# Eight weight chunks in other column orders, and weight slots 64 bytes further apart

## What is computed

```python
h = rms_norm(x, g_mix[l])
proj = h @ w_in[l]
q, k, v, z, f, scal, gates = jnp.split(proj, SPLIT_POINTS, axis=-1)
...
gate_a, gate_f = jnp.split(jax.nn.sigmoid(gates), N_BRANCHES, axis=-1)
x = x + (gate_a * y_a + gate_f * y_f) @ w_o[l]
```

## Time and profile before

| | before |
|---|---|
| median of 2 runs | 2401.64 us (2400.94 to 2402.33) |
| profiled execution, its span | 2400.5 us |
| TensorE busy | 2376.3 us, 99% |
| VectorE busy | 1773.2 us, 74% |
| ScalarE busy | 1027.0 us, 43% |
| GpSimd busy | 267.3 us, 11% |
| DMA | 475.16 MB, 198 GB/s on average |

### The profile page before, as it was taken

One profiled execution on the slowest core, in us unless ns is written; L12 is line 12 of the kernel. 1 busy time (PEld: TensorE's weight loads), 2 busy tenths in 40 slices (PEclk: granted clock), 3 DMA queues, 4 the chain that ended last, 5 costly groups with the idle time before them and its releaser, 6 DMA issues.

```text
span 2400.5 us, 29952 instructions
## 1 busy us (share of the span) xinstructions
PE 2376.3 (99%) x12546; PEld 1946.3 (81%) x12546; DVE 1773.2 (74%) x2054; ACT 1027.0 (43%) x849; POOL 267.3 (11%) x226
## 2 busy tenths in 40 slices
PE   8999999999999999999999999999999999999998
PEld 7888888878888888888888888777777788888886
DVE  6585568557697887786766789989999967458865
ACT  5453345334344544444444435444434444544432
POOL 1002201210000000000000000055555400000000
PEclk9999999999999999999999999999999999999999
DMA  7343354347655555555555556665556586566753
GB/s 264 136 167 133 141 185 166 118 155 259 259 193 189 195 194 211 194 193 193 193 193 193 193 210 217 203 237 186 193 192 201 180 299 241 184 231 236 258 195 140
DMA packets 84230, 475.16 MB, mean 198 GB/s; under 512 B 8704, under 2 KB 8832, under 8 KB 32512
## 3 DMA queue, kind: packets, MB, share of 16 engines
q1 hardware_dynamic: 84096, 473.25, 55.7%
HBM read 450.15 MB, written 23.07 MB: 197 GB/s over the span
## 4 chain that ended last, share of the span: by engine, by line
PE 90%; DVE 6%; DMA 2%; issue 1%; ACT 1%; DVEq 0%; SPq 0%; ACTq 0%
PE acc L2179 28%; PE acc L2182 27%; PE acc L2185 27%; PE banks L2324 2%; DVE w_lo L1257 1%; PE banks L2373 1%; DMA raw<-in_w 1%; DVE convT L1577 1%; DVE padT L1304 1%; PE banks L2440 1%; PE banks L2453 1%; ACT w_hi L796 1%; PE banks L2196 0%; PE banks L2493 0%; PE banks L2475 0%
## 5 line engine op out<-in xcount | busy, mean ns | idle before, releaser
L1257 DVE TENSOR_TENSOR w_lo<-raw,w_hi 128x2048 fp32r<-128x2048 f32 x394 | 909.1, 2309 | 387.2 <-ACT w_hi L796 384.2
L796 ACT ACTIVATE w_hi<-raw 128x2048 fp32r<-128x2048 f32 x394 | 752.6, 1915 | 667.6 <-DMA raw<-in_w 667.2
L2179 PE MATMUL acc<-w_hi,a_hi 128*128 128x512 f32 x2112 | 839.5, 397 | 5.8 <-DVE w_lo L1257 2.6
L2182 PE MATMUL acc<-w_lo,a_hi 128*128 128x512 f32 x2112 | 824.9, 391 | 0.0
L2185 PE MATMUL acc<-w_hi,a_lo 128*128 128x512 f32 x2112 | 824.4, 390 | 0.0
L2179 PEld LDWEIGHTS acc<-w_hi,a_hi 128*128 128x128 f32 x2112 | 397.4, 188 | 105.6 <-issue 16.9
L2185 PEld LDWEIGHTS acc<-w_hi,a_lo 128*128 128x128 f32 x2112 | 397.4, 188 | 84.9 <-DVE a_lo L1293 0.3
L2182 PEld LDWEIGHTS acc<-w_lo,a_hi 128*128 128x128 f32 x2112 | 397.8, 188 | 78.6
L2179 PE MATMUL acc<-w_hi,b_hi 128*128 128x512 f32 x928 | 361.8, 390 | 0.0
L2185 PE MATMUL acc<-w_hi,b_lo 128*128 128x512 f32 x928 | 361.3, 389 | 0.0
L2182 PE MATMUL acc<-w_lo,b_hi 128*128 128x512 f32 x928 | 361.2, 389 | 0.0
(11 more groups left out here) (354 smaller groups left out, 1688.9 us busy)
## 6 DMA issues: line engine op xcount, KB each, us to landing
raw<-in_w SPq DMA_DIRECT2D x395, 1024.0 KB, 4.8
spilled<-stage SPq DMA_DIRECT2D x72, 256.0 KB, 5.8
gate_in<-spilled SPq DMA_DIRECT2D x20, 512.0 KB, 5.7
x_rows<-in_x SPq DMA_DIRECT2D x4, 512.0 KB, 8.5
x_rows<-in_x SPq DMA_DIRECT2D x1, 2048.0 KB, 9.3
mem_rows<-in_mem SPq DMA_DIRECT2D x2, 1024.0 KB, 6.6
spilled<-stage_b SPq DMA_DIRECT2D x8, 256.0 KB, 5.8
out<-y_rows SPq DMA_DIRECT2D x3, 512.0 KB, 2.7
```

Source lines behind the costliest of these rows:

```text
L796: act.activation(w_hi[:, n % HIGH, :], raw[:, n % RAW, :], ACT.Copy)\
L1257: dve.tensor_tensor(w_lo[:, n % RAW, :], raw[:, n % RAW, :], w_hi[:, n % HIGH, :].bitcast(F32), ALU.subtract).then_inc(lo_split, 1)
L2179: pe.matmul(o, hi[:, tk], wh, start=first, stop=False)
L2182: pe.matmul(o, hi[:, tk], wl, start=False, stop=False)
```

## The change

Eight chunks, all of w_gate_f and w_gate_a, get another order of their columns within a unit, made on the host by `laid_in_blocks`. TensorE reads them with an access pattern that undoes it (`moving`), so that the result stands in `acc` in the old order. What ScalarE, VectorE and the DMA do to a unit is as before. With a block of i elements, block b of slice k starts at element 4 i b + i k of the unit, so one slice is read as 512 / i runs of i elements, and the starts of two runs are 4 i elements apart.

| chunk | w_gate_f 0 | 1 | 2 | 3 | w_gate_a 0 | 1 | 2 | 3 |
|---|---|---|---|---|---|---|---|---|
| order | 32 | 2 | halves | back | 1 | 64 | 256 | 16 |
| one slice is read as | 16 runs of 32, 512 bytes apart | 256 pairs, 32 bytes apart | elements 0, 256, 1, 257, ... | 512 elements with step -1 | 512 elements, 16 bytes apart | 8 runs of 64 | 2 runs of 256 | 32 runs of 16, 256 bytes apart |

In the second part the slots of `raw`, `w_lo` and `w_hi` become 2064 elements long, of which 2048 are used, so that they begin 8256 bytes apart. All that is allocated behind them moves up by up to 512 bytes per partition.

```diff
+BLOCKS = {("w_gate_f", 0): 32, ("w_gate_f", 1): 2, ("w_gate_f", 2): "halves", ("w_gate_f", 3): "back",
+          ("w_gate_a", 0): 1, ("w_gate_a", 1): 64, ("w_gate_a", 2): 256, ("w_gate_a", 3): 16}
...
-        ctx.enter_context(nc.sbuf_tensor("arena", [P, 52984], F32))
+        ctx.enter_context(nc.sbuf_tensor("arena", [P, 53112], F32))
...
-        raw = take("raw", [P, RAW, UE])
-        w_lo = at("w_lo", 0, [P, RAW, UE], F32R)
-        w_hi = take("w_hi", [P, HIGH, UE], F32R)
+        raw = take("raw", [P, RAW, UE + 16])[:, :, 0:UE]
+        w_lo = at("w_lo", 0, [P, RAW, UE + 16], F32R)[:, :, 0:UE]
+        w_hi = take("w_hi", [P, HIGH, UE + 16], F32R)[:, :, 0:UE]
...
-                    wh = w_hi[:, n % HIGH, k * NW:(k + 1) * NW]
-                    wl = w_lo[:, n % RAW, k * NW:(k + 1) * NW]
+                    wh = moving(w_hi[:, n % HIGH, :], k, block_order(name, col))
+                    wl = moving(w_lo[:, n % RAW, :], k, block_order(name, col))
...
+def block_order(name, n):
+
+    return BLOCKS.get((name, n))
+
+
+def moving(x, k, block):
+
+    if block is None:
+        return x[:, k * NW:(k + 1) * NW]
+    if block == "back":
+        return x[:, (k + 1) * NW - 1:k * NW - 1 if k else None:-1]
+    if block == "halves":
+        return x[:, k * NW:(k + 1) * NW].rearrange("p (z j) -> p j z", z=2)
+    return x.rearrange("p (b k i) -> p k b i", k=KU, i=block)[:, k]
+
+
+def laid_in_blocks(units, block):
+
+    u = units.reshape(-1, P, KU, NW)
+    if block == "back":
+        return np.ascontiguousarray(u[:, :, :, ::-1]).reshape(units.shape)
+    if block == "halves":
+        return np.ascontiguousarray(u.reshape(-1, P, KU, NW // 2, 2).swapaxes(3, 4)).reshape(units.shape)
+    return np.ascontiguousarray(u.reshape(-1, P, KU, NW // block, block).swapaxes(2, 3)).reshape(units.shape)
...
-    w = np.concatenate([units[name][n * u:(n + 1) * u] for name, n, u, _ in CHUNKS])
+    piece = lambda name, n, u: units[name][n * u:(n + 1) * u]
+    w = np.concatenate([piece(name, n, u) if block_order(name, n) is None else
+                        laid_in_blocks(piece(name, n, u), block_order(name, n)) for name, n, u, _ in CHUNKS])
```

More of the change, by code:

```diff
@@ L399, in region @@
         def region(name, kb, shape, dt=F32):
-            assert dr + kb * KB + int(np.prod(shape[1:])) * 4 <= 52984 * 4, name
+            assert dr + kb * KB + int(np.prod(shape[1:])) * 4 <= 53112 * 4, name
             return at(name, dr + kb * KB, shape, dt)
```

## The result

| | before | after |
|---|---|---|
| median | 2401.64 us | 2475.84 us (2474.19 to 2477.48, 2 runs) |
| ratio | | 1.0308, 95% interval 1.0291 to 1.0325 |
| span of the profiled execution | 2400.5 us | 2475.7 us |

What follows compares the result with a forecast made beforehand. TensorE, busy 2376.3 of 2400.5 us, was taken to bound the kernel. Pairs at +18.9 us, single elements and halves at +58.2 each, all else 0, summed to +135.3 on 2401.6: 2537 us, range 2420 to 2580.

Steps and rivals of the forecast that it cites:

- (a): Slots of raw, w_lo and w_hi 8256 bytes apart instead of 8192: taken as 0 us.
- 13.4 ns left over per matmul: Weight matmuls start 226.7 ns apart; 512 columns at 2.4 GHz need 213.3; the rest was read as TensorE's port at its limit.
- The rival that had an effect of (a): Shifted slots free the 13.4 ns in 9504 weight matmuls: 127 us faster, 2274 us alone, 2410 with the sum; chance 0.02.
- the rival of no effect: Moving operand fetched ahead or through a port so wide that steps don't matter: 2401.6 us; chance 0.13.
- (b): Five orders in the gate chunks, blocks of 256, 64, 32, 16 and backwards: as many fetches as before, 0 us.
- (c): Blocks of 2 in w_gate_f 1: 256 fetches of 1.6 ns, +196 ns for each of 96 matmuls, +18.9 us.
- (d): Blocks of 1 in w_gate_a 0: 512 fetches of 1.6 ns, +606 ns for each of 96 matmuls, +58.2 us.
- (e): Halves in w_gate_f 2: +58.2 us, if no fetched piece is kept while the other is read.
- half pace: TensorE's port serves one place per 0.83 ns: pairs free, blocks of 1 and halves +20.4 us each, 2442.6 us; chance 0.27.
- the neighbour at 2422: Variant near half pace: only blocks of 1 pay, since in halves both pieces are kept, 2422 us; chance 0.06.
- The likeliest case: TensorE's fetch price of 1.5 to 1.67 ns per new place, with or without a lower clock, 2528 to 2565 us; chance 0.38.
- The neighbour at 2480: Variant near half pace: blocks of 1 at 606 ns, the rest by half pace, 2480 us; chance 0.05.

Runs made afterwards that it cites:

- swapped twin: Blocks of 2 in w_gate_a 0 taken 0, 8, 1, 9 instead of 0, 1, 8, 9, slots at multiples of 8192 bytes: 218 ns per matmul against 461 to 462.
- z = 4: One survey chunk, slots at multiples of 8192 bytes: a slice read as 4 elements 128 apart, then their neighbours: 283 ns, contiguous 227.
- z = 2 with runs of 2: One survey chunk, slots at multiples of 8192 bytes: a slice read from two places 256 elements apart, two elements at a time: 333 ns, contiguous 227.
- z = 8: One survey chunk, slots at multiples of 8192 bytes: a slice read as 8 elements 64 apart, then their neighbours: 487 ns, contiguous 227.

## Why the prediction was right or wrong

**What bounds the kernel** was read rightly. What was added to the weight matmuls reached the end; idle time stayed at 22.6 us, near the 24 that were named. The distance of two starts was the right price: 0.461 us in the slow chunks, where the latency is 0.64 us.

**(a), the slots, at 0** failed. It cost 30.7 us alone, 41% of the change. The step that failed is the reading of the 13.4 ns left over per matmul. I took them for a port at its limit, which the 216 ns of halves bear out, and did not ask what a shift of 64 bytes does to a port at its limit. The rival that had an effect of (a) had it with the other sign. The argument against it, that the distance does not grow with VectorE's work, was right about VectorE and said nothing of TensorE's own second read, the weight load, which is there in every matmul. The trace before had a sign of it: the rival of no effect says that all matmuls are 226.7 ns apart, but those with m_hi and m_lo are 232.4 ns apart, and their latency of 396 ns against 390 stands in the earlier trace rows. What the Trainium skill says under "Who interferes with whom", in "SBUF — State Buffer", that TensorE does not wait on another engine, is not touched by this; but the same section calls its moving and stationary reads independent, and the measurements speak against that: + 51 us with no moving read moved, and 232.4 against 226.7 ns by the stationary operand alone.

**(b)** was right within 3 us: long runs and the backward order cost up to 16 ns per matmul.

**(c), blocks of 2, at + 196 ns** was mis-sized a little: 461 - 226.7 = 234 ns, 22.5 us and not 18.9. Word for word, two hits on a line would have made it free; the trace does not agree. Read for each lane, the rule of the Trainium skill ("SBUF — State Buffer", SBUF "cachelines" under Door 1) fits this order and its swapped twin: at least two hits, but each lane needs its own. It does not fit z = 4 (283 ns) and z = 2 with runs of 2 (333).

**(d), blocks of 1, at + 606 ns** failed: 234 ns, 22.5 us and not 58.2. The step was to carry VectorE's 1.6 ns per new place over to TensorE. With each element in a new line it passes a column per 0.9 ns. The rival of half the pace had this one right: it said 427 ns, measured 461.

**(e), halves, at + 58.2 us** failed in its sign: - 1.0 us. I assumed that a piece which is left is lost. Nothing in the trace before read two places in turn; half pace had it slow too (+ 20.4 us), and the neighbour at 2422 and no effect had it free at best. That it could be faster than contiguous reading was on no list.

From the sum of 135.3 us, 35.7 go off for (d) and 59.2 for (e), and 30.7 for (a), 3.6 for (c) and about 2.5 for (b) come on top: 77.2 us, against 74.2 measured. Errors of both signs happened to leave the time inside the range: that was luck, and the mechanism of the prediction, VectorE's price per new place, did not hold for TensorE. The likeliest case with its own range of 2528 to 2565 was wrong, and so was "half pace" with 2442.6, in which (c) was free, (e) was slow and (a) nothing. The neighbour at 2480 is nearest by its number alone: it has (d) at 606 ns and (e) slow. Also, the 2% that the prediction takes for the least that can be told from no change is too much; the intervals here are 0.2% to either side.

## What to carry to other kernels

For float32r matmuls of 512 columns, choose the order of the moving operand's columns so that elements 0, 2, 4, 6 of the stream share 16 bytes, and 1, 3, 5, 7 another 16: 216 ns per matmul in the place of 227 for the contiguous order, by an access pattern and a matching layout alone, and alike in the three placements of the buffers that were tried. In an order that steps without this interleaving keep runs of at least four elements, since runs of one or two cost 1.2 to 2.1 times as much. Judge an edit that only moves buffers by the distances of starts in chunks that it doesn't touch; here it was worth 1.3 to 2.1%.

## What was not expected of the hardware

- Elements 0, 256, 1, 257, ... 1 KB apart are read faster (216 ns) than neighbours (226.7). The places of the blocks of 2 take 218 ns when read as 0, 8, 1, 9 and 461 when read as 0, 1, 8, 9.
- In the contiguous order the distance between matmuls depends on where the stationary operand begins against the moving one: 226.7 to 233.5 ns for the same instructions, by the place modulo 256 bytes where w_hi and w_lo stand alike.
- Half the pace of columns over 96 matmuls left the granted clock at 1.00.
- Eight places in turn (z = 8, 487 ns) are slower than sixteen to sixty-four (431 to 434), which nothing here explains.
